# A two-layer hybrid encoder on one core: attention's small TensorE work gathered behind every second unit

## The reference

```python
for l in range(DEPTH):                      # 2 layers, x is (1, 256, 2048) float32
    h = rmsnorm(x, norm1_g[l])
    proj = h @ w_in[l]                      # 2048 x 4352
    aq, ak, av, bq, bk, bv, cq, ck, cv = jnp.split(proj, splits, axis=-1)
    out_a = mixer_chunked_relbias(...)      # 8 heads of 64, relative bias
    out_b = mixer_swa_sinks(...)            # 16 heads of 64, 2 key/value heads, sinks, rotary
    out_c = mixer_diff(...)                 # 4 heads, two softmax maps each, rotary
    x = x + jnp.concatenate([out_a, out_b, out_c], axis=-1) @ w_out[l]
    h2 = rmsnorm(x, norm2_g[l])
    x = x + jnp.square(jax.nn.relu(h2 @ w_up[l])) @ w_down[l]
```

## Time and profile before

| what | value |
|---|---|
| median of three runs | 2096.11 us (2094.85 to 2096.46) |
| the profiled execution's own time | 2095.73 us |
| its span (first to last instruction) | 2093.6 us |
| TensorE matmul, weight load | busy 2078.8 us (99%), 1740.4 us (83%) |
| VectorE, ScalarE, GpSimd | busy 1279.5 us (61%), 995.4 us (48%), 177.7 us (8%) |
| mean granted TensorE clock | 0.999 |

### The profile page before, as it was taken

How to read it: one execution, slowest core, us unless ns; L and a number is a source line. 1 busy time by engine, 2 the same in 40 slices (tenths; PEclk the granted TensorE clock), 3 DMA queues, 4 the chain that set the end, 5 groups by cost and what they waited for, 6 DMA issues and landing times.

```text
span 2093.6 us, 26442 instructions
## 1 busy us (share of the span) xinstructions
PE 2078.8 (99%) x10602; PEld 1740.4 (83%) x10602; DVE 1279.5 (61%) x1645; ACT 995.4 (48%) x1328; POOL 177.7 (8%) x181
## 2 busy tenths in 40 slices
PE   8999999999999999999999999999999999999999
PEld 7887778888888888888888877888888888888887
DVE  6768566565565556556676675665555655565664
ACT  5557644443443444344455576444434434443443
POOL 2344210000000000000023522000000000000000
PEclk9999999999999999999999999999999999999999
DMA  7666765666666666666566567656666666666663
GB/s 257 177 201 177 200 195 178 188 191 194 189 190 193 190 189 192 193 189 191 182 185 189 166 179 205 200 181 191 191 191 191 191 191 191 189 194 191 190 192 121
DMA packets 207737, 396.48 MB, mean 189 GB/s; under 512 B 14750, under 2 KB 21760, under 8 KB 207616
## 3 DMA queue, kind: packets, MB, share of 16 engines
q1 hardware_dynamic: 202784, 379.75, 59.1%
q0 software_dynamic: 4032, 14.68, 3.7%
q10 hardware_dynamic: 800, 0.37, 0.1%
HBM read 377.95 MB, written 2.12 MB: 182 GB/s over the span
## 4 chain that ended last, share of the span: by engine, by line
PE 98%; DVE 1%; issue 0%; DMA 0%; ACT 0%; SPq 0%; ACTq 0%
PE psum L475 39%; PE psum L495 22%; PE psum L479 20%; PE psum L498 12%; PE psum L505 1%; PE psum L565 1%; PE psum L591 1%; PE psum L552 1%; PE psum L550 1%; DVE w_lo L850 1%; PE psum L593 0%; DMA x<-in_x_dram 0%; ACT w_hi L670 0%; DVE probs L1012 0%; PE psum L650 0%
## 5 line engine op out<-in xcount | busy, mean ns | idle before, releaser
L850 DVE TENSOR_TENSOR w_lo<-raw_ring,w_hi 128x1024 fp32r<-128x1024 f32 (+1 forms) x692 | 854.6, 1236 | 745.2 <-ACT w_hi L670 744.3
L670 ACT CAST w_hi<-raw_ring 128x1024 fp32r<-128x1024 f32 (+1 forms) x720 | 749.9, 1042 | 1014.8 <-PE psum L479 624.9
L495 PE MATMUL psum<-xt,w_hi 128*128 128x512 f32 x2048 | 512.9, 392 | 0.0
L475 PE MATMUL psum<-w_hi,ht_hi 128*128 128x512 f32 x1280 | 502.1, 392 | 0.0
L475 PE MATMUL psum<-w_hi,ht_lo 128*128 128x512 f32 x1280 | 498.6, 390 | 0.0
L495 PEld LDWEIGHTS psum<-xt,w_hi 128*128 128x128 f32 x2048 | 368.8, 189 | 66.3
L479 PE MATMUL psum<-w_lo,ht_hi 128*128 128x512 f32 x1280 | 342.5, 389 | 0.0
L498 PEld LDWEIGHTS psum<-xt,w_lo 128*128 128x128 f32 x2048 | 279.4, 190 | 19.9
L498 PE MATMUL psum<-xt,w_lo 128*128 128x256 f32 x2048 | 285.6, 282 | 0.0
L475 PEld LDWEIGHTS psum<-w_hi,ht_hi 128*128 128x128 f32 x1280 | 240.3, 188 | 51.7 <-issue 3.0
L475 PE MATMUL psum<-w_hi,xt 128*128 128x512 f32 (+1 forms) x1152 | 282.1, 387 | 0.0
(11 more groups left out here) (130 smaller groups left out, 988.7 us busy)
## 6 DMA issues: line engine op xcount, KB each, us to landing
raw_ring<-in_w_up_dram SPq DMA_DIRECT2D x256, 512.0 KB, 3.6
raw_ring<-in_w_down_dram SPq DMA_DIRECT2D x256, 512.0 KB, 3.6
raw_ring<-in_w_in_dram SPq DMA_DIRECT2D x128, 512.0 KB, 4.3
raw_ring<-in_w_out_dram SPq DMA_DIRECT2D x64, 512.0 KB, 4.2
w_lo<-raw_ring POOLq DMA_DIRECT2D x28, 512.0 KB, 5.1
raw_ring<-in_w_in_dram SPq DMA_DIRECT2D x16, 256.0 KB, 2.8
x<-in_x_dram SPq DMA_DIRECT2D x4, 512.0 KB, 7.3
out_dram<-x SPq DMA_DIRECT2D x3, 512.0 KB, 2.8
```

The source lines that it names most:

```text
L475: pe.matmul(bank[r][:, 0:cols], t[:, kt, r * P:(r + 1) * P], w_hi[:, slot, j, 0:cols], start=first and j == 0 and n == 0, stop=False, skip ...
L495: pe.matmul(bank[:, f, :], w_hi[:, w, j, f * P:(f + 1) * P], both, start=kt == 0, stop=False, skip_group_check=True)
L670: act.copy(w_hi[:, u % AHEAD, :, 0:cols], raw_ring[:, u % RAWS, :, 0:cols]).then_inc(hi_ready, 1)
L850: dve.tensor_tensor(w_lo[:, u % AHEAD, :, 0:cols], raw_ring[:, u % RAWS, :, 0:cols], w_hi[:, u % AHEAD, :, 0:cols].bitcast(F32), ALU.subtr ...
```

## The change

The small work of attention is put behind every second unit, in the order values, first transpose, scores, second transpose, `use_t`. A pair's exponentials are at the step of its scores, both transposes two units behind the scores (C's one transpose four), the values four (C: eight). On ScalarE copies of values come ahead of the hi split, and an eviction comes behind the exponentials. On VectorE `copy_probs` and `pair_lo` come ahead of the lo split. The last four pairs and some of `T_USE` and `NORM_AT` move by two steps.

```diff
-POOL_SCALES = {61: 6, 69: 7}
+POOL_SCALES = {63: 6, 71: 7}
...
-PAIR_AT = {**{25 + 4 * h: h for h in range(4)}, **{49 + 2 * n: 4 + n for n in range(8)}, **{71 + 2 * n: 12 + n for n in range(4)}}
-EXPS = {s + 1: n for s, n in PAIR_AT.items()}
+PAIR_AT = {**{25 + 4 * h: h for h in range(4)}, **{49 + 2 * n: 4 + n for n in range(8)}, **{73 + 2 * n: 12 + n for n in range(4)}}
+EXPS = {s: n for s, n in PAIR_AT.items()}
...
-PROBS_T = {**{s + 5: n for s, n in PAIR_AT.items() if n < 4},
-           **{s + 3 + m: 2 * n - 4 + m for s, n in PAIR_AT.items() if n >= 4 for m in range(2)}}
-VALUES = {s + (7 if n < 4 else 5): n for s, n in PAIR_AT.items()}
+PROBS_T = {**{s + 4: [n] for s, n in PAIR_AT.items() if n < 4},
+           **{s + 2: [2 * n - 4, 2 * n - 3] for s, n in PAIR_AT.items() if n >= 4}}
+VALUES = {s + (8 if n < 4 else 4): n for s, n in PAIR_AT.items()}
...
-         59: ("qk", 6, 0), 61: ("qk", 6, 1), 65: ("mixC", 7), 67: ("qk", 7, 0), 69: ("qk", 7, 1)}
+         61: ("qk", 6, 0), 63: ("qk", 6, 1), 65: ("mixC", 7), 69: ("qk", 7, 0), 71: ("qk", 7, 1)}
...
-           58: (6, 0), 60: (6, 1), 66: (7, 0), 68: (7, 1)}
+           60: (6, 0), 62: (6, 1), 68: (7, 0), 70: (7, 1)}
...
-STATS_AT = {8 * c + 7 + 1: c for c in QK}
+STATS_AT = {8 * c + 8 + (c > 5): c for c in QK}
@@ TensorE, mix @@
-                if s in PROBS_T:
-                    transpose_probs(pl, PROBS_T[s])
+                fills = PROBS_T.get(s, [])
+                if fills:
+                    transpose_probs(pl, fills[0])
                 if s in PAIR_AT:
                     scores(pl, PAIR_AT[s])
+                if len(fills) == 2:
+                    transpose_probs(pl, fills[1])
                 if s in T_USE:
                     use_t(pl, s)
@@ ScalarE, mix @@
+                if s in VALUES:
+                    copy_values(pl, VALUES[s])
                 split_hi(pl, u, PROJ[u // UPC][2] if u < PU else CW)
...
-                if evicts:
-                    if s in VALUES:
-                        copy_values(pl, VALUES[s])
-                    if s in T_USE and T_USE[s][0] == "qk":
-                        copy_qk(pl, s)
-                    evict_proj(pl, s // UPC)
-                if s in VALUES and not evicts:
-                    copy_values(pl, VALUES[s])
-                if s in T_USE and T_USE[s][0] == "qk" and not evicts:
+                if s in T_USE and T_USE[s][0] == "qk":
                     copy_qk(pl, s)
                 if s in EXPS:
                     for m in range(2):
                         exponentials(pl, 2 * EXPS[s] + m)
+                if evicts:
+                    evict_proj(pl, s // UPC)
@@ VectorE, mix @@
-                if s in STATS_AT:
+                if s in STATS_AT and STATS_AT[s] < 6:
                     head_sums(pl, STATS_AT[s])
...
+                fills = PROBS_T.get(s, [])
+                if fills:
+                    copy_probs(pl, fills[0])
+                if s in VALUES and VALUES[s] >= 4:
+                    pair_lo(pl, VALUES[s])
...
-                if s in PROBS_T:
-                    copy_probs(pl, PROBS_T[s])
                 if s in PAIR_AT:
                     for m in range(2):
                         mask_and_max(pl, 2 * PAIR_AT[s] + m)
-                if s in VALUES and VALUES[s] >= 4:
-                    pair_lo(pl, VALUES[s])
+                if len(fills) == 2:
+                    copy_probs(pl, fills[1])
+                if s in STATS_AT and STATS_AT[s] >= 6:
+                    head_sums(pl, STATS_AT[s])
```

More of the change, by code:

```diff
@@ L544, in scores @@
                 else:
-                    q, k, b, kb, ready = qk_t[0], qk_t[1], n - 12, n - 12, 69
+                    q, k, b, kb, ready = qk_t[0], qk_t[1], n - 12, n - 12, 71
                 pe.wait_ge(t_free, pl.at(T_USES, T_BEFORE + T_NUMBER[ready] + 1))
```

## The result

The changed kernel takes 2127.52 us (median of 4 runs, 2127.03 to 2127.70), the kernel before 2095.52 beside it (2094.85 to 2096.46). The ratio is 1.0152 [1.014, 1.0165], 32 us slower. The profiled execution took 2127.7, its span 2125.8, 32.2 more than before.

The account below looks back on a forecast made before the run. TensorE's queue, 99% busy, was taken as the bound. Per layer 15.9 of waits + 1.6 for the clock - 0.7 - 1.6 = 15.2, twice 30.4, less 0.7: 29.7 on 2095.7 gives 2125.4 us, range 2109 to 2133.

Parts of the forecast that it names:

- The steady groups: Groups 53, 55, 61 and 63: TensorE waits for weighted probabilities ahead of the first transpose, 0.35 to 0.4 each.
- at 75: Group behind one without values or transposes: TensorE arrives early and waits 1.05 for splits and weighting.
- Evictions: Groups 57 and 65: exponentials plus a chunk's eviction on ScalarE delay the hi split, costing 2.6 and 2.3.
- The two copies between transposes: At 65 and 81, without scores between, the second transpose waits for the copy from their shared bank: 0.9 each.
- Group 51: TensorE waits for pair 4's weighting, behind exponentials, hi split and a VectorE slowed by GpSimd's rotary work: 5.2 per layer.
- Lo split 54 took 2.32: At group 51, VectorE's lo split beside GpSimd was taken to last 2.32, as before the change, not 1.2.
- Sum of waits: All new TensorE waits in the groups from 51 to 81, summed per layer: 15.9.
- The clock: Granted clock falls behind the long wait at 51, slowing transposes and next hi block: 1.6 per layer.
- TensorE's own saving: Gathering saves returns to big work on TensorE: 0.05 in each of 14 groups, 0.7 per layer, bounds 0 to 2.8.
- the old waits gone: The former wait at unit 53 disappears, saving 1.6 per layer, and a third wait saves 0.7 once.
- VectorE passes the rotary work: Rival: pair 4's split and weighting fall between GpSimd operations, wait at 51 is 2.5, clock holds: 2117; chance 0.2.
- Faster: Rival: the weighting is always there in time, only the gains of 5.3 stand: 2090; chance 0.07.

Follow-up runs that it names:

- The first experiment: Changed kernel with VectorE's weighting of B and A pairs one step earlier, ahead of the lo split of the unit between scores and transpose: 2105.78 us.
- the second experiment: Changed kernel with ScalarE's evictions of chunks 6 and 7 one step later, at steps 56 and 64 behind the hi split: 2117.71 us.
- the fourth experiment: Changed kernel with the C pairs' transposes one unit later, behind units 30, 34, 38 and 42: 2130.43 us.
- mended kernels: Changed kernel with earlier weighting, later evictions and C transposes, second transposes of 65 and 81 later, and variants for pairs 4 and 5: 2097.74 to 2100.78 us.
- the last experiment: Mended kernel with pair 4's second transpose at 52 and mixed rows' transposes at 66, plus pair 5's weighting back at step 53: 2097.74 us.
- the fifth experiment: Changed kernel with weighting, eviction and C edits, pair 4's scores at 48, values at 53, second transposes of 65 and 81 later: 2099.5 us.

## Why the prediction was right

2125 was forecast, 2127.5 measured, inside the range, and by the mechanism that was named. Point by point:

- **The steady groups.** Forecast 0.35 to 0.4 each in 53, 55, 61, 63; measured 0.33 more time from lo block to transpose. At 59 0.8 against 0.75, at 75 1.0 against 1.05. The first experiment removes all of them by the order alone. At 77 and 79 0.13 against 0.15, but 79 in the first layer was 0.6, not explained here. The waits view names the weighted probabilities 21 times where some 24 were forecast.
- **Evictions.** 2.4 at 57 against 2.6, 2.4 at 65 against 2.3. Shown by the second experiment. The two copies between transposes cost 0.96 each against 0.9.
- **Group 51: the term that was mis-sized.** Forecast 5.2 (164.0 + 2.3 + 3.1 against 164.1 is 5.3), measured 4.25. The step "Lo split 54 took 2.32" did not carry over: it came ahead of a GpSimd product, not behind it. In the fourth experiment it came second again, and the wait was 5.26. The rule of the Trainium skill (SBUF — State Buffer, "Who interferes with whom"), from which the prediction worked out 5.0, was applied there to a split that comes second as well; the rule itself, whoever starts first goes on and the other waits, agrees with the rows (split 1.22 and product 1.80 here, 1.78 and 0.72 in the fourth experiment, where a wait for the whole of the other one would give about 1.9 both times).
- **A wait that was not foreseen.** 0.7 per layer at unit 29 (0.86 from start to start) for a C pair, whose exponentials now stand ahead of the hi splits. Only the pairs of B and A had been worked through.
- **Sum of waits.** Start to start, 16.2 in the first layer and 15.7 in the second, against 15.9: the missing 0.95 at 51 is made up by the wait at 29 and, in the first layer, the odd 0.6.
- **The clock.** Forecast 1.6 per layer. Behind 51 it fell in both layers and cost 2.9 and 2.3, since the small work stands at the lower clock too and not the hi block alone; behind 65 it fell in the second layer, 1.6. Together 6.8 against 3.2, as much as the page's busy TensorE grew.
- **TensorE's own saving.** Forecast 0.7 per layer. Layer 1 is 15.2 longer in the trace, where waits 16.2, clock 2.9 and the old waits gone (-2.3) make 16.8; layer 2 16.5, where they make 18.0. So 1.5 per layer, within the bounds but twice the value taken. Stretches without waits show somewhat less directly: the eight units from 57 take 0.23 less than before in all mended kernels, some 0.06 per group; in the last experiment units 57 to 85 take 0.7 and 1.1 less, the old wait at 79 left out; units 29 to 49 take 0.1 less in the fourth. That makes about 1 per layer; where the rest lies is not shown.
- **The start** took 0.4 more. In the traces of this study that stretch differs by over 1 us with no change made to it; its one wait for issue is 3.8 to 4.8.

Against the forecast of 29.7 that is 0.1 more of waits, 3.6 more of clock, 1.6 more saved and 0.4 at the start: 32.2. The waits' sum hides an error of 1.9 at 51 and one of the same size the other way elsewhere, and 3.6 too little for the clock stands against 1.6 too little saved, so the exactness of the total is partly luck.

The rival "VectorE passes the rotary work" failed as stated: the split did pass, but sums and scalings did not (0.69 and 2.17). "Faster" fell with the first plain group. That gathering itself costs TensorE time is refuted by the stretches without waits in the mended kernels' traces, not by their times, none of which is under the one before. The kernel of the last experiment loses in one place what it gains in the others: in its trace units 29 to 57, with the same work in them, are 2.3 longer than before in each layer (the wait of 2.05 at 53 and the clock behind it, less the old wait of 1.6), all behind them 1.6 and 1.1 shorter. Whether another order keeps pairs 4 and 5 clear of GpSimd's rotary work, and so is faster than before, stays open.

## What to carry to other kernels

Gathering small work saves a queue that is 99% busy very little (here 1 to 1.5 us per layer), and it shortens the time that the other engines have between two stations of a chain (here from three units to two). Before such a change, write down for one steady group when each station ends, and then look for the places where another job stands ahead of the chain (an eviction, a copy, GpSimd beside VectorE): here they cost 2.4 and 4.3 where a plain group lost 0.33. Move the chain's steps in all engines' orders together with it; moving the weighting by one step gave back two thirds of the loss.

## What the runs showed of the hardware

- A split of 1.22 beside a GpSimd product is decided by which starts first: 0.01 ahead it took 1.22 and the product 1.80 for 0.72; 0.02 behind it 1.78; 0.06 behind a longer product 2.32. With the shift of 0.03 between the first two the wait at 51 grew by 1.2 us, half of it in the split and half in the scalings behind it.
- Four scalings of 1.01 took 2.17 to 2.78 beside GpSimd's rotary products, and the sums 0.68 to 0.87 for 0.15. The copy out of PSUM was not slowed (0.54 at 168.07 in the fifth experiment for its usual 0.55).
- The clock's fall did not follow the length of the wait alone. Behind 4.1 and 5.26 it came every time, and the transpose that ended the wait already took 0.90 instead of 0.55. Behind 2.8 it came every time too, behind 2.3 to 2.5 in some groups of a kernel and not in others with the same wait, and behind 2.05 in both layers of the last experiment. Behind the waits of 2.8 and less it began with that transpose in some places and some pieces later in others: in the last experiment two pieces behind it in the first layer and at once in the second. So a wait's price was its length or its length and 1.3 to 2.9 more, and cutting one wait did not keep the clock from falling behind the same place or another.
